# Moving linear attention's small products between the input products of a mixer, and its output blocks into the forgetting loop, on one core

## The reference, cut to what matters

```
proj = rms_norm(h) @ w_in
fq, fk, fv, ff, gq, gk, gv, glr, gr = split(proj)        # widths 512 512 512 8 256 256 512 16 512
# forgetting attention, 8 heads of 64, 256 positions, swept in two blocks t of 128 queries
s[t, s] = norm(fq) . norm(fk) / 8 + c[t] - c[s] + causal mask,  c = cumsum(log_sigmoid(ff + b))
fox = softmax(s) @ fv
# gated linear attention, 4 heads, keys 64, values 128, chunks of 64 positions
bc = cumsum(log_sigmoid(glr @ w_gate2 + b) / 16) within a chunk
A = tril((gq * exp(bc)) (gk * exp(-bc))^T);  dS = (gk * exp(bc_last - bc))^T gv
state_c = decay * state_(c-1) + dS_c
o = A @ gv + (gq * exp(bc)) @ state
gla = rms_norm(o) * gain * silu(gr)
h = h + concat(fox, gla) @ w_out
# cross-attention, 4 heads of 256, 256 memory rows
h = h + softmax(norm(q) . norm(k) / 16) v @ wo
h = h + relu(rms_norm(h) @ w1)^2 @ w2
```

## Time and profile before

| | us |
|---|---|
| median of 3 runs | 1755.61 |
| lowest, highest | 1754.98, 1767.9 |
| profiled execution | 1768.46 |
| its span | 1766.7 |
| PE busy | 1339.0 (76%) |
| DVE, ACT, POOL busy | 492.0, 347.5, 152.1 |
| granted clock, mean | 0.867 |

### The profile page before, as it was taken

One profiled execution on the slowest core, in us unless ns is written; L12 is line 12 of the kernel. 1 busy time (PEld: TensorE's weight loads), 2 busy tenths in 40 slices (PEclk: granted clock), 3 DMA queues, 4 the chain that ended last, 5 costly groups with the idle time before them and its releaser, 6 DMA issues.

```text
span 1766.7 us, 18071 instructions
## 1 busy us (share of the span) xinstructions
PE 1339.0 (76%) x7746; PEld 785.0 (44%) x7746; DVE 492.0 (28%) x706; ACT 347.5 (20%) x513; POOL 152.1 (9%) x142
## 2 busy tenths in 40 slices
PE   5989875685675785599666657556568989899999
PEld 2744541231231231199411212112116857789997
DVE  1369540010100000356401001001006632445553
ACT  1111420010010010133100000000005632444442
POOL 1043000000000000100000000000004150440000
PEclk9999978898887897799788888778869966999999
DMA  9999749999999999984399999999998511435530
GB/s 372 394 388 356 296 158 423 417 412 422 417 421 422 413 420 422 401 306 170 128 422 422 422 422 421 422 422 422 423 391 300 190 48 64 161 109 183 183 112 25
DMA packets 110000, 561.83 MB, mean 318 GB/s; under 512 B 8516, under 2 KB 9908, under 8 KB 54126
## 3 DMA queue, kind: packets, MB, share of 16 engines
q1 hardware_dynamic: 105880, 551.76, 77.7%
q0 software_dynamic: 2208, 8.36, 1.3%
q10 hardware_dynamic: 1846, 0.75, 0.2%
HBM read 557.69 MB, written 3.16 MB: 317 GB/s over the span
## 4 chain that ended last, share of the span: by engine, by line
PE 40%; DMA 31%; DVE 3%; ACT 2%; SPq 1%; issue 1%; POOL 0%; DVEq 0%; ACTq 0%; POOLq 0%
PE ps L1855 22%; DMA ring<-in_moe_w_down 13%; DMA ring<-in_moe_w_up 12%; PE ps L2105 8%; DMA ring<-in_moe_w_gate 5%; PE ps L1840 3%; PE ps L2119 1%; SPq L472 1%; PE ps L2339 1%; DMA ring<-in_w_in 1%; PE ps L2152 1%; PE ps L2354 0%; PE ps L2327 0%; PE ps L2329 0%; ACT ring_parts L587 0%
## 5 line engine op out<-in xcount | busy, mean ns | idle before, releaser
L2105 PE MATMUL ps<-ring,scratch 128*32 128x512 f32 x3072 | 469.7, 768 | 284.1 <-DMA ring<-in_moe_w_up 129.1
L2105 PEld LDWEIGHTS ps<-ring,scratch 128*32 128x32 f32 x3072 | 127.1, 136 | 601.0 <-issue 598.4
L1855 PE MATMUL ps<-ring_parts,scratch_parts 128*128 128x512 f32 x656 | 190.8, 410 | 5.1 <-DVE xT_parts L1163 1.4
L1855 PE MATMUL ps<-scratch_parts,ring_parts 128*128 128x256 f32 x704 | 145.7, 282 | 0.0
L1855 PEld LDWEIGHTS ps<-ring_parts,scratch_parts 128*128 128x128 f32 x656 | 125.2, 193 | 38.3 <-issue 7.4
L587 ACT ACTIVATE ring_parts<-ring 128x2048 fp32r<-128x2048 f32 x56 | 106.1, 1919 | 93.7 <-PE ps L1855 87.4
L1855 PEld LDWEIGHTS ps<-scratch_parts,ring_parts 128*128 128x128 f32 x704 | 115.9, 190 | 0.3
L438 DVE TENSOR_TENSOR ring_parts<-ring,ring_parts 128x2048 fp32r<-128x2048 f32 x44 | 100.7, 2289 | 53.4 <-ACT ring_parts L587 52.1
L1456 DVE TENSOR_TENSOR scratch<-ps,gate_bc 128x512 f32<-128x512 f32 x16 | 10.3, 686 | 298.2 <-PE ps L2105 298.2
L1448 DVE TENSOR_TENSOR scratch<-scratch,ps 128x1024 f32<-128x1024 f32 x8 | 9.8, 1222 | 286.7 <-PE ps L2105 286.7
L1855 PE MATMUL ps<-xT_parts,ring_parts 128*128 128x256 f32 x288 | 80.9, 281 | 1.3 <-DVE xT_parts L1154 1.3
(11 more groups left out here) (379 smaller groups left out, 1559.8 us busy)
## 6 DMA issues: line engine op xcount, KB each, us to landing
ring<-in_moe_w_gate SPq DMA_DIRECT2D x64, 2048.0 KB, 28.6
ring<-in_moe_w_up SPq DMA_DIRECT2D x64, 2048.0 KB, 25.8
ring<-in_moe_w_down SPq DMA_DIRECT2D x64, 2048.0 KB, 31.6
ring<-in_ada_w SPq DMA_DIRECT2D x24, 2048.0 KB, 12.9
ring<-in_mlp_w SPq DMA_DIRECT2D x16, 2048.0 KB, 8.3
ring<-in_sc_w_in SPq DMA_DIRECT2D x6, 2048.0 KB, 20.9
ring<-in_w_in SPq DMA_DIRECT2D x6, 2048.0 KB, 16.9
ring<-in_xattn_wkv SPq DMA_DIRECT2D x4, 2048.0 KB, 29.8
```

Source lines behind the costliest of these rows:

```text
L1855: last = mm(out, lhs[x], rhs[y], start=start and n == 0, stop=stop and n == 2)
L2105: last = mm(ps[32 * j:32 * j + 32, banks[half], :], src[:, k, CAP * j:CAP * (j + 1)], w[j * RUN // EG][:, j % (EG // RUN), col:col + 512], ...
```

## The change

What it does, by engine:

- **Order of chunks**: w_gv, w_gr, w_fv in place of w_fv, w_gv, w_gr, on every engine.
- **PE**: the key transposes and A go between w_fk and w_gv; dS between the two halves of w_gr, with the transposes of fq and fk; NB and linear attention's output before w_fv. For t=1 the product from A is one of 128 rows instead of two of 64. The gated output is transposed inside w_fv (wait for `mix_rows` 1 at block 4 of its second half). The blocks of w_out move from heads 8 to 15 of the loop to heads 0 to 7.
- **VectorE**: AT and klrow before the head norms; the copies of fT after the states; two of w_out's subtractions (second halves) before the loop; the division of block t=0 inside the loop at n = 10 (`FOX_AT`).
- **ScalarE**: Silu of gr, a one-column Exp, the squares and linear attention's high columns before the loop; the first halves of w_out's high copies inside it, at n = 9 and 11.
- **GpSimd**: the gate product before the mask; `gr` in place; instead of both chunks of w_out it splits their first halves, in the loop. Ahead of the short convolution it waits for both normalised rows.
- **Cross-attention**: the product of the maximum with the scale is a ScalarE Copy in `x_probs` instead of a VectorE product.
- Buffers and PSUM banks move to fit (fT out of xT, go in place of gv, NB0 in scratch; FS, FO, WO, GO and the banks of the norm).

```diff
-          ("w_small", 1), ("w_gqk", 1), ("w_fq", 1), ("w_fk", 1), ("w_fv", 1), ("w_gv", 1), ("w_gr", 1),
+          ("w_small", 1), ("w_gqk", 1), ("w_fq", 1), ("w_fk", 1), ("w_gv", 1), ("w_gr", 1), ("w_fv", 1),
...
-        FS, FTB, FO = (1, 2), (6, 7), (0, 4)
-        WO = ((3, 5), (1, 2))
-        GLA_AT = 5
+        FS, FTB, FO = (4, 5), (6, 7), (1, 2)
+        WO = ((0, 3), FS)
+        FT = ((4, 5), (6, 7))
+        FOX_AT = FOXH + 2
...
-        def low(eng, ops, i):
-            for n, w, lo, hi in halves(i):
+        def low(eng, ops, i, only=(0, 1)):
+            for half, (n, w, lo, hi) in enumerate(halves(i)):
+                if half in only:
...
@@ scalar @@
-            act.wait_ge(sem("go_sb"), 1)
+            high(FIRST["w_out"], (1,))
+            scaled_rows("w_gr", gr, FO, ACT.Silu)
+            nc.scalar.activation(sm[:, 208:209], ones[:, 0:1], ACT.Exp)
+            high(FIRST["w_out"] + 1, (1,))
             for t in range(NT):
+                act.wait_ge(sem("go_sb"), t + 1)
                 for hd in range(GLAH):
...
+            columns_high(8, WO[0], gla_x[0])
+            scaled_rows("w_fv", fv, FO)
...
-                if n == GLA_AT:
-                    columns_high(8, WO[0], gla_x[0])
+                if n in (FOXH + 1, FOXH + 3):
+                    high(FIRST["w_out"] + (n - FOXH) // 2, (0,))
...
             def x_probs(n):
                 act.wait_ge(sem("xa_max"), n + 1)
+                act.wait_ge(sem("head_rstd"), n // 4 + 3)
+                link(nc.scalar.activation(sm[:, 64 + n:65 + n], sm[:, 64 + n:65 + n], ACT.Copy, scale=sm[:, 48 + n:49 + n]))
...
@@ gpsimd @@
             pool.wait_ge(sem("w_high"), n + 1)
+            pool.wait_ge(sem("norm_rows"), 2 * NORMED.index("mix1") + 2)
             nc.gpsimd.tensor_tensor(lo, w, hi.bitcast(F32), ALU.subtract).then_inc(sem("w_split"), 1)
...
-            low(pool, nc.gpsimd, FIRST["w_out"])
-
...
+            pool.wait_ge(sem("go_sb"), 2)
+            link.mark(nc.gpsimd.tensor_tensor(gr, gr, go, ALU.mult))
...
-            low(pool, nc.gpsimd, FIRST["w_out"] + 1)
+            nc.gpsimd.tensor_tensor(NB[:, :, P:N], NB[:, :, P:N], mask, ALU.add).then_inc(sem("nb"), 1)
+            for j in range(2):
+                low(pool, nc.gpsimd, FIRST["w_out"] + j, (0,))
...
@@ vector @@
+            for j in range(2):
+                low(dve, nc.vector, FIRST["w_out"] + j, (1,))
+            columns_low("w_out", 0, WO[0], gla_x[1], gla_x[0])
+
+            def fox_rows(t):
+                dve.wait_ge(sem("fx_pv"), FOXH * (t + 1))
...
-                dve.wait_ge(sem("head_rstd"), g + 3)
...
-                        link(nc.vector.tensor_reduce(sm[:, 64 + n:65 + n], ps[:, n % 2, 0:N], AX.X, ALU.max, negate=True))
-                        nc.vector.tensor_tensor(sm[:, 64 + n:65 + n], sm[:, 64 + n:65 + n], sm[:, 48 + n:49 + n], ALU.mult)\
+                        nc.vector.tensor_reduce(sm[:, 64 + n:65 + n], ps[:, n % 2, 0:N], AX.X, ALU.max, negate=True)\
...
@@ tensor @@
+            split_rows(FIRST["w_fq"], x, (4, 5))
+            split_rows(FIRST["w_fk"], x, (6, 7))
...
+            (key transposes, A)
+            pe.wait_ge(sem("fqk"), 2)
+            split_rows(FIRST["w_gv"], x, (4, 5))
+            pe.wait_ge(sem("AT"), 2)
+            split_half(FIRST["w_gr"], 0, x, FO).then_inc(sem("w_halves_used"), 1)
...
+            (dS, transposes of fq and fk)
+            split_half(FIRST["w_gr"], 1, x, FO).then_inc(sem("w_halves_used"), 1)
             pe.wait_ge(sem("cols"), 8)
...
+            (NB)
+            pe.wait_ge(sem("states"), 1)
+            for hd in range(GLAH):
+                for c in range(2):
+                    o = slice(GCH * c, GCH * (c + 1))
+                    mm(gla_out(0, hd, o), AT[:, 0, hd, o], gv[:, 0, GDV * hd:GDV * (hd + 1)], start=True, stop=(c == 0))
+                last = gla_chunk(1, hd)
+            last.then_inc(sem("go_ps"), 1)
+            pe.wait_ge(sem("nb"), 2)
+            for hd in range(GLAH):
+                mm(gla_out(1, hd), AT[:, 1, hd, :], gv[:, 1, GDV * hd:GDV * (hd + 1)], start=True, stop=False)
+                for c in (2, 3):
+                    last = gla_chunk(c, hd)
+            last.then_inc(sem("go_ps"), 1)
+
+            pe.wait_ge(sem("values"), 4)
+            i = FIRST["w_fv"]
+            split_half(i, 0, x, FO).then_inc(sem("w_halves_used"), 1)
+            for b in range(8):
+                if b == 4:
+                    pe.wait_ge(sem("mix_rows"), 1)
+                    row_transposes(gr, WO[0], range(4))
+                last = split_block(i, 1, b // 4, b % 4, x, FO[b // 4])
...
-                if n >= FOXH:
-                    w_out_block(0, n - FOXH)
+                if n < FOXH:
+                    w_out_block(0, n)
```

More of the change, by code:

```diff
@@ L238, in build @@
         NB = at(6912, h=FOXH, n=N)
-        NB0 = rows[:, :, 0:512].rearrange("p t (h n) -> p t h n", n=P)
+        NB0 = [at(off, h=FOXH // 2, n=P) for off in (0, 6144)]
         fv = at(8960, t=NT, e=512)
@@ L401, in halves @@
         def halves(i):
+            j = i - FIRST["w_out"]
             for half in range(2):
                 n = 2 * (i - N0 - 1) + half
+                if j in (0, 1):
+                    n = 2 * (FIRST["w_out"] - N0 - 1) + 2 * (1 - half) + j
                 hi = w_hi[n % 4]
@@ L865, in _ @@
                 whole(act, name)
                 for t in range(NT):
[L867 to L871, removed]
+                    nc.scalar.activation(dst[:, t, :], pb(banks[t]), func, scale=row_scale[:, t:t + 1]).then_inc(sem("values"), 1)
@@ L1629, in _ @@
             nc.vector.tensor_tensor(gkT, gkT, ex[:, 0], ALU.mult).then_inc(sem("gl_klast"), 1)
-            low(dve, nc.vector, FIRST["w_fv"])
+            low(dve, nc.vector, FIRST["w_gv"])
+            dve.wait_ge(sem("gl_klast"), 1)
+            link.mark(nc.vector.memset(AT, 0.0))
+            dve.wait_ge(sem("kl_ps"), 1)
+            nc.vector.tensor_copy(klrow.rearrange("p t r e -> p (t r e)"), pb(0)).then_inc(sem("klrow"), 1)
+            dve.wait_ge(sem("first_params_in"), 6 * 16)
+            link.wait()
+            for w in range(2):
+                dve.wait_ge(sem("A_ps"), w + 1)
+                for t in range(NT):
+                    last = nc.vector.copy_predicated(AT[:, t].rearrange("p (r w) c -> p w r c", w=2)[:, w],
+                                                     glam[:, :].unsqueeze(1).broadcast_to([P, 2, P]),
+                                                     pb(1 + w)[:, 256 * t:256 * t + 256].rearrange("p (r c) -> p r c", r=2))
+                last.then_inc(sem("AT"), 1)
             sums = sm[:, 0:32].rearrange("p (t w h) -> p w t h", t=NT, w=2)
@@ L2268, in _ @@
-            pe.wait_ge(sem("values"), 4)
+            split_rows(FIRST["w_fq"], x, (4, 5))
+            split_rows(FIRST["w_fk"], x, (6, 7))
+            pe.wait_ge(sem("gate_abs"), 1)
+            pe.wait_ge(sem("gqk"), 2)
+            pe.wait_ge(sem("gl_klast"), 1)
+            for t in range(NT):
+                for r in range(2):
+                    last = nc.tensor.transpose(ps[:, 0, P * (2 * t + r):P * (2 * t + r + 1)], gkT[:, r, P * t:P * (t + 1)], ident)
+            last.then_inc(sem("kl_ps"), 1)
@@ new lines, in _ @@
+            for w in range(2):
+                for t in range(NT):
+                    for r in range(2):
+                        s = slice(64 * w, 64 * w + 64)
+                        last = mm(ps[:, 1 + w, P * (2 * t + r):P * (2 * t + r + 1)], kdec[s, r, P * t:P * (t + 1)],
+                                  gqT[s, r, P * t:P * (t + 1)], start=True, stop=True)
+                last.then_inc(sem("A_ps"), 1)
+            pe.wait_ge(sem("fqk"), 2)
+            split_rows(FIRST["w_gv"], x, (4, 5))
@@ new lines, in _ @@
+            pe.wait_ge(sem("AT"), 2)
+            split_half(FIRST["w_gr"], 0, x, FO).then_inc(sem("w_halves_used"), 1)
+            pe.wait_ge(sem("gate_abs"), 2)
+            pe.wait_ge(sem("klrow"), 1)
+            pe.wait_ge(sem("values"), 2)
+            for chunks, bank in (((0, 2), 0), ((1,), 3)):
+                for c in chunks:
+                    s, t = slice(GCH * (c % 2), GCH * (c % 2) + GCH), c // 2
+                    for hd in range(GLAH):
+                        r, w = hd // 2, hd % 2
+                        col = GDV * (2 * r + c // 2) if bank == 0 else GDV * r
+                        last = mm(ps[64 * w:64 * w + 64, bank, col:col + GDV], klrow[s, t, r, 64 * w:64 * w + 64],
+                                  gv[s, t, GDV * hd:GDV * (hd + 1)], start=True, stop=True)
+                last.then_inc(sem("dS_ps"), 1)
@@ L2334, in fox_scores @@
+            last.then_inc(sem("w_halves_used"), 1)
             def fox_scores(n):
```

182 lines of the change are left out of this document (64 added, 118 removed).

## The result

The changed kernel takes 1751.15 us (median of 20, 1749.8 to 1759.7). The kernel before, timed 20 times beside it, takes 1768.06 (1754.5 to 1777.8), not the 1755.61 of the three runs shown ahead. The ratio is 0.9931, 95% interval 0.9909 to 0.9954: about 12.2 us faster, under one per cent. My time of 1738.5 was too low and its range (to 1751.0) just misses; "within 1%" had 0.47. The profiled executions, 1768.46 and 1750.33, differ by 18.1 us; I had worked out 17.1.

A forecast was written before the change was run, and what follows sets the result against it. PE was taken to bound the mixer and cross-attention, much of it at half clock. Mixer -8.6, cross-attention -5.0 and short convolution -3.5 gave -17.1 us, taken off the 1755.6 median: 1738.5 us, own range 1733 to 1744, all cases 1727 to 1751.

The forecast's parts named there:

- within 1%: Whole kernel: the outcome of a time changed by less than one per cent, 17.6 us, given a chance of 0.47.
- the sum: Whole kernel: mixer -8.6, cross-attention bias -5.0 and short convolution -3.5 us, together -17.1 us.
- the two small parts: Cross-attention bias on ScalarE, -5.0 us, and GpSimd's wait ahead of the short convolution's first split, -3.5 us.
- Up to the loop: Mixer from 1359.43 us to the forgetting loop: 84.6 us, so the loop starts 4.7 us later than before.
- the wait: PE inside w_fv waits for `mix_rows` 1 from GpSimd's chain: 3.7 us, bounds 0 and 5.9.
- take turns: After go_sb, VectorE's w_out subtractions and GpSimd's chain alternate, adding 2 x 2.3 us to the chain.
- the half clock behind it: Mixer, after PE's pause for `mix_rows` 1: about one more stretch of half clock, +1.7 us.
- The loop: Forgetting loop in the mixer: 31.1 us, full clock in t=0 and half from 3.8 us into t=1, -10.8 us.
- A head of t=0: Forgetting loop's first half: 1.45 us per head at full clock; eight and the entry make 13.0 us.
- w_out's start at half clock: Behind the loop: w_out's blocks start at half clock, costing +2.2 us.
- Full clock through the loop: Rival for the forgetting loop: the clock stays full, t=1 takes 13.4 instead of 18.1 us, total 1731.6; chance 0.25.

The follow-up runs named there:

- its part alone: The changed kernel with its cross-attention bias back on VectorE and no GpSimd wait ahead of the short convolution: median 1760.56 us, ratio 0.9981 to the kernel before.
- the early subtractions: The changed kernel with VectorE's two subtractions of w_out's second halves moved ahead into its idle times: median 1743.84 us, ratio 0.9876 to the kernel before.
- the late subtractions: The changed kernel with VectorE's two subtractions of w_out's second halves waiting for mix_rows 1: four times at 1759 to 1760.4 us, ratio 0.9991 to the kernel before.
- the second profile of before: The kernel before, unchanged, run and profiled again: the profiled execution took 1755.21 us, its loop 33.3 us.
- the bias alone: The kernel before with only the product of the cross-attention's maximum with the scale moved to ScalarE: ratio 0.9989.
- GpSimd's wait alone: The kernel before with only GpSimd's wait for both normalised rows ahead of the short convolution: ratio 0.9965.

## Why the prediction was wrong, step by step

- **The step that failed** is the one that turns the sum into a time: "That execution is slower than the median of the runs (1755.6; one of three was at 1767.9) in parts that the change doesn't touch, so I take it off the median." It was slower in the very loop that I was costing: 46.6 us at half clock against 33.3 where the clock rises at 1454. The 1755.6 already lacked 12.9 us of the 15.5 that I took off for the loop. Nothing in the trace supported "in parts that the change doesn't touch"; three times at two levels 12.9 us apart, in a kernel with a loop that runs at half clock without a gap, should have been a warning and a rival of its own. Without it the times would have come out: 17.1 us off the 1768.06 that is before's median of 20 is 1751.0, for 1751.15. From the profiled execution itself the sum gives 1751.4; its measured counterpart is 1750.3.
- Against each of before's two kinds of loop (the difference of 8.5 us left out) the change is worth -4.8 us (1755.6 to 1750.8) and -17.5 (1768.3 to 1750.8). With 12 of 20 executions in the slower one, 0.4 x 4.8 + 0.6 x 17.5 = 12.4 us, beside the measured 12.2. Of these, 8 to 8.5 us are the two small parts, in every execution. The rest, about 4 us, is the mixer: at the end of w_out's products its part alone is 3.9 us behind the profile of before with the fast loop and 9.4 ahead of the one with the slow loop, and its ratio (0.9981, interval 0.9949 to 1.0013) does not even show it. The change puts in place of a mixer that was fast 8 times in 20 one that lies in between, each time.
- **Up to the loop**: +4.7 forecast, +5.1 measured; the wait 3.7 for 4.25 us. That VectorE and GpSimd take turns is shown by their rows above and by the early and the late subtractions. The wait and the half clock behind it, 3.7 + 1.7 in the forecast, are what the early subtractions won: 6.6 us (85.0 less 78.4).
- **The loop**: 31.1 forecast, 31.0 measured, but by two errors that cancel. A head of t=0 costs 1.59 us for my 1.45 (the distance of two block rows), so that t=0 with the entry takes 13.5 us for my 13.0. The clock fell 6.2 us into t=1 for my 3.8, but at full clock its heads cost about 2.0 us for my 1.7 (PE waits 0.50 and 0.84 us for ScalarE there), and t=1 takes 17.4 us for my 18.1.
- **The two small parts**: -5.0 and -3.5 forecast; -4.8 and -3.3 measured alone. Beside the changed mixer the bias is worth more: without it 283.1 us lie behind the loop, with it 276.6. PE's stop is followed by more half clock there, a mean of 0.74 from 1520 to 1533, where the second profile of before has 0.87 (1516 to 1529).
- **Behind the loop** I had +2.2 for w_out's start at half clock and -5.0 for the bias, -2.8; measured -4.2. The +2.2 was too much: the first 12 products took 4.14 us, 3.04 in the earlier trace rows, so 1.1.
- **Rivals.** Full clock through the loop (0.25) did not come in the change; spreading the blocks made it come. The Trainium skill ("TensorE: Matmul & The Clock Gate", Part 1, what is actually happening) says that the clock's state depends on where in a running activity window the work falls, that this varies from run to run, and that the cost is under 1% of a typical kernel. The two profiles of before agree that it varies from run to run, and stand at the edge of the last: equal instructions, equal times to 0.3 us up to 1454, then 13.3 us apart in one loop, 0.75% of the kernel. That the place in a window decides, no run here shows.

**What stays open.** Why the rise at 1454 comes in one execution and not in another was not settled: extra work ahead of it or behind it changes whether it lasts and how often, and no run shows what tips it. Nor does the place of the clock's fall ahead of the loop tell it: counted from w_fq's start it is at 63.9 us in the two profiles of an unchanged loop where the rise came (before again, the bias alone) and at 64.0 and 63.8 where it did not (before, GpSimd's wait alone). The difference of 8.5 us in both kernels is the clock between 100 and 300 us; what tips it was not followed.

## What to carry to other kernels

Before a sum made on one profiled execution is taken off a median, ask where that execution differs from the median; if the times lie in groups, profile the other group first, for a loop at half clock may be one side of a coin. Where a small-product loop holds back dense work that has no place of its own, spread it evenly over the loop rather than bunch it: the same eight blocks in the second half, the first half or at every second head gave 1759.5, 1750.8 and 1743.3 us, in the lowest group of each. Put a two-operand instruction of one of VectorE and GpSimd into that engine's idle time, not beside the other's critical chain, and look where the wait goes: taking it away at the wrong place made the kernel 9 us slower.

## What the runs showed of the hardware that I had not expected

- In the kernel before, adding six useless products in heads 5, 6 and 7 took the groups at 1768 and 1777 away; adding the first two alone took those at 1755 and 1764 away.
- PE 100% busy for 37 us stays at a granted clock of 0.5 (with the blocks back in t=1), and 97% busy for 24 us at 1.00 (spread): how busy PE is does not tell the clock.
- Subtractions of 128x2048 on VectorE and a 128x1024 product on GpSimd side by side took 6.69 (two of them) and 4.32 us; apart, 4.56 and 2.38.
